# Gate 1 and the delta-rule mixer's gate as seven-product blocks, and what moves for it

## The reference, cut to what matters

```python
mod = jax.nn.silu(c) @ P['w_ada'] + P['b_ada']            # 12 groups of 512 columns
h = _rmsnorm(x, P['norm_mix_w']) * (1.0 + sc_m) + sh_m
proj = h @ P['w_in']     # u_a, qkv_b, z_b, a_b, b_b, x_c, gate_c, z_d, xbc_d, dt_d, gate_raw
# delta rule, chunks of 64 in the reference, 128 in the kernel; g, beta per token and head
kk = k k^T ; lhs = I + strict(beta * kk * decay) ; sol = lhs^-1 [v beta, k beta exp(g)]
u = sol_v - sol_k S ; o = (q exp(g)) S + (q k^T * decay) u ; S = S exp(g_end) + k_end^T u
o = o * rsqrt(mean(o*o) + EPS) * P['gdn_norm_w'] * silu(z)          # z_b is the mixer's gate
gates = sigmoid(gate_raw)             # four gates of 1024 channels: gate0 to gate3
out = sum(gates * branches) @ P['w_out']
```

## Time and profile before

| | |
|---|---|
| median of runs | 2577.1 us (2575.58 to 2579.7) |
| the profiled execution | 2580.41 us, span 2578.6 us |
| PE busy | 2415.3 us, 94% |
| DVE / ACT / POOL busy | 1124.6 / 787.4 / 545.0 us |
| PE, gate 1 (L660) | 151.5 us busy, 768 records of 192 columns |
| PE, units (L704) | 671.2 us busy, 2688 records of 288 columns |
| PE, tiles (L541) | 515.3 us busy, 1584 records of 384 columns |

### The profile page before, as it was taken

How to read it: one execution, slowest core, us unless ns; L and a number is a source line. 1 busy time by engine, 2 the same in 40 slices (tenths; PEclk the granted TensorE clock), 3 DMA queues, 4 the chain that set the end, 5 groups by cost and what they waited for, 6 DMA issues and landing times.

```text
span 2578.6 us, 41253 instructions
## 1 busy us (share of the span) xinstructions
PE 2415.3 (94%) x16732; PEld 1619.7 (63%) x16732; DVE 1124.6 (44%) x1802; ACT 787.4 (31%) x1507; POOL 545.0 (21%) x524
## 2 busy tenths in 40 slices
PE   5999899999999999999999999999987999989994
PEld 3555888885677777776777755555464444434443
DVE  4355555553362565984959912333452111101115
ACT  3132222221123222336477531110142222222224
POOL 0000000003466344665744500000000000000003
PEclk9999999999999999999999999999997999999997
DMA  7000123203111111411101252223036466767436
GB/s 326 33 33 33 46 81 111 79 29 111 70 33 49 47 63 65 166 33 51 72 31 56 80 223 106 106 106 114 1 139 270 152 238 245 296 236 268 154 131 232
DMA packets 71908, 304.20 MB, mean 118 GB/s; under 512 B 9693, under 2 KB 35877, under 8 KB 48421
## 3 DMA queue, kind: packets, MB, share of 16 engines
q1 hardware_dynamic: 59620, 267.98, 27.7%
q0 software_dynamic: 8928, 22.03, 2.5%
q10 hardware_dynamic: 3168, 11.54, 1.1%
HBM read 699.18 MB, written 63.71 MB: 296 GB/s over the span
## 4 chain that ended last, share of the span: by engine, by line
PE 79%; DMA 8%; DVE 5%; ACT 4%; issue 2%; SPq 1%; POOL 1%; ACTq 0%; DVEq 0%; POOLq 0%
PE psum L704 22%; PE psum L541 20%; PE psum L1666 8%; DMA arena<-in_moe 7%; PE psum L1524 4%; PE psum L1650 4%; PE psum L660 4%; PE psum L1241 2%; ACT arena L1990 1%; PE psum L570 1%; PE psum L1127 1%; PE psum L1103 1%; PE psum L1635 1%; PE psum L1229 1%; PE psum L1461 1%
## 5 line engine op out<-in xcount | busy, mean ns | idle before, releaser
L704 PE MATMUL psum<-arena 128*128 128x288 f32 x2688 | 671.2, 410 | 12.7 <-ACT arena L785 8.4
L704 PEld LDWEIGHTS psum<-arena 128*128 128x128 f32 x2688 | 508.0, 191 | 163.5 <-issue 12.2
L541 PE MATMUL psum<-arena 128*128 128x384 f32 x1584 | 515.3, 488 | 5.7 <-issue 2.9
L541 PEld LDWEIGHTS psum<-arena 128*128 128x128 f32 x1584 | 300.9, 190 | 219.4 <-issue 9.6
L1666 PE MATMUL psum<-arena 128*32 128x256 f32 x5632 | 326.3, 388 | 36.2 <-DMA arena<-in_moe 35.0
L1666 PEld LDWEIGHTS psum<-arena 128*32 128x32 f32 x5632 | 179.3, 112 | 169.5 <-DMA arena<-in_moe 38.1
L2180 POOL TENSOR_TENSOR arena<-arena,cst 128x288 f32<-128x288 f32 (+1 forms) x204 | 180.5, 888 | 51.9 <-ACT cst L779 22.5
L2108 ACT ACTIVATE arena<-psum 32x512 f32<-32x512 f32 x174 | 102.4, 589 | 230.7 <-PE psum L1650 229.2
L1650 PE MATMUL psum<-arena 128*32 128x512 f32 x1408 | 162.5, 600 | 7.8 <-DMA arena<-in_moe 7.2
L779 ACT ACTIVATE cst<-psum 128x288 f32<-128x288 f32 x192 | 78.9, 412 | 249.0 <-PE psum L704 243.4
L660 PE MATMUL psum<-arena 128*128 128x192 f32 x768 | 151.5, 332 | 0.0
(11 more groups left out here) (563 smaller groups left out, 2902.3 us busy)
## 6 DMA issues: line engine op xcount, KB each, us to landing
arena<-in_moe SPq DMA_DIRECT2D x532, 1024.0 KB
arena<-in_ada SPq DMA_DIRECT2D x12, 2048.0 KB, 8.8
arena<-gate_raw SPq DMA_DIRECT2D x8, 2304.0 KB, 8.0
gate_raw<-arena SPq DMA_DIRECT2D x96, 144.0 KB, 1.8
arena<-in_gate SPq DMA_DIRECT2D x12, 1024.0 KB, 5.2
y_rows<-arena ACTq DMA_DIRECT2D x22, 512.0 KB
arena<-in_br SPq DMA_DIRECT2D x8, 1024.0 KB, 9.6
y_save<-arena SPq DMA_DIRECT2D x3, 2304.0 KB, 6.9
```

The lines of the kernel that those rows point to most:

```text
L541: last = nc.tensor.matmul(pset(s)[:, n, :], w[:, kk, :], src[:, kk, n * N3:(n + 1) * N3], start=(kk == 0), stop=(kk == K - 1))
L704: last = nc.tensor.matmul(bank(6 + i % 2)[:, 0:NQ4], w[:, k, :], x[:, k, :], start=(k == 0), stop=(k == 3))
```

## The change: what it does

- Gate 1 and zb become units. The loop's fill is now the first token half (h = 0) of gates 1, 3 and 2: 12 units, 336 matmuls of 288 columns, one pair of tiles and half of the tokens at a time. The second halves come later, so these weights are loaded twice. Units in all: 48 before, 60 after.
- GpSimd works from the end of the first stage on: three forms of the first token half, after all modulation rows, then the one in place when the last qkv tile is filled, then sums for every unit of the loop, the unit's additions, and the squares' addition (k's place += v's place) of chunks 0 to 7. After the loop it makes the second half's forms, when the store of the prompt's state is done; VectorE copies the first half's forms to their later place.
- The modulation groups 4 to 11 are made in the first stage, one at each of the qkv tiles 2 to 9: its rows ahead of the tile, its columns ahead of the tile's last third (`pe_tile` now yields there).
- The short sequences' state is loaded over v's place in QKV.
- Behind the loop come zb, xbc and two units of gate 2; zd moves into the middle loop with the second halves of gates 1 and 3, its silu after chunks 2, 3, 5, 6. In the LRU stage one unit stands behind each of the four tiles. ScalarE's eviction of ua's first pair waits for two LRU tiles and not for four.
- ScalarE squares the outputs of the chunk before ahead of the exponentials, and its evictions lag by one product in the first solves (LAGGED).

```diff
-STREAM = [("xbc", 0), ("xbc", 1), ... ("gate0", 2), ("gate0", 3)]
-UNITS = [(a, p, h) for a, p in STREAM for h in range(2)]
+VISITS = [("gate%d" % k, p, (0,)) for k in (1, 3, 2) for p in range(4)]
+LOOP_UNITS = len(VISITS)
+VISITS += [("zb", 0, BOTH), ("zb", 1, BOTH)] + [("xbc", p, BOTH) for p in range(4)] + [("gate2", 0, (1,)), ("gate2", 1, (1,))]
+VISITS += [("zd", 0, BOTH), ("zd", 1, BOTH)] + [("gate%d" % k, p, (1,)) for k in (1, 3) for p in range(4)]
+VISITS += [("xc", 0, BOTH), ("xc", 1, BOTH), ("gc", 0, BOTH), ("gc", 1, BOTH), ("gate2", 2, (1,)), ("gate2", 3, (1,))]
+VISITS += [("ua", 0, BOTH), ("ua", 1, BOTH)] + [("gate0", p, BOTH) for p in range(4)]
...
-        counts = [("start", 13 if last else 17), ("ops", 4)]
+        counts = [("start", 4 if last else 12), ("ops", 2 if last else 3)]
...
-            counts += [("turn%d" % st, 2), ("right%d" % st, 1)]
-            counts += [("step%d_%d" % (st, i), 1) for i in range(st == SOLVE - 1 and not last, steps - (last and st == len(STEPS[c])))]
-        counts += [("w", 2), ("o", 2)] if last else [("w", 0), ("o", 0)]
-        counts += [("head%d" % h, 8) for h in range(GH)] if last else [("next", 2)]
+            counts += [("turn%d" % st, 1 if last else 2), ("right%d" % st, 1)]
+            counts += [("step%d_%d" % (st, i), 0 if last else 1)
+                       for i in range(st == SOLVE - 1 and not last, steps - (last and st == len(STEPS[c])))]
+        counts += [("w", 1 if last else 2), ("o", 1 if last else 0)]
+        counts += [("head%d" % h, 5) for h in range(GH)] if last else [("next", 4)]
...
+LAGGED = ("turn1", "right1", "turn2", "right2", "right3") + tuple("step%d_%d" % (st, i) for st in (1, 2, 3) for i in range(3))
...
 # TensorE, first stage
             for m in range(12):
+                t = m - 2
+                ada = 0 <= t < LATE
+                if ada:
+                    pe.wait_ge(s_awl, 16 * (t + 1))
+                    if t:
+                        pe.wait_ge(s_mod, t)
+                    if t == 5:
+                        pe.wait_ge(s_zero, 2)
+                    ada_rows(pe, 7 if t < 5 else 6, AWL)
...
-                    pe_tile(pe, "qkv", m, w[:, m % 4], HT, KD)
+                    for _ in pe_tile(pe, "qkv", m, w[:, m % 4], HT, KD):
+                        if ada:
+                            pe.wait_ge(s_aev, ADA_EARLY + t + 1)
+                            ada_cols(7 if t < 5 else 6, 0, adaL)
...
 # TensorE, in a unit
+                if u == LOOP_UNITS:
+                    pe.wait_ge(t_moved, 1)
+                if new:
                     pe.wait_ge(u_sums, FORMS[(2, h)])
-                if h == 0:
+                if FIRST[u]:
                     pe.wait_ge(u_sums, sums_no(n, 2))
...
 # ScalarE
+                if c:
+                    act_out_squares(c - 1)
                 act.wait_ge(c_diff, c + 1)
...
+                take(max(GDN_COUNT[(c, tag)] // 4 - (tag in LAGGED) - at, 0))
+                dst = QKV[:, 8:12, c * P:(c + 1) * P] if c != NC7 - 1 else hd(late_sq, 4)
...
+            take(7 * LOOP_UNITS + 7 - at)
+            act_root(S, "gdn_ss", 0, rt_n, 1.0 / P, rms_eps)
...
+                if c in (2, 3, 5, 6):
+                    act_silu_y("zd", (2, 3, 5, 6).index(c))
...
 # GpSimd
-            wait_phase(pool, 2)
+            pool.wait_ge(s_arow, ADA)
+            forms(0, loop_forms)
+            wait_fill(pool, "qkv", 11)
+            form_in_place(0)
+            for _ in sums(0):
+                pass
             for u in range(len(UNITS)):
+                if u < LOOP_UNITS:
+                    for c in range(NC7):
+                        if u == -(-(GDN_COUNT[(c, "next")] + 4) // YIELDS):
+                            add_squares(c)
+                if u == LOOP_UNITS:
+                    wait_phase(pool, 2)
+                    pool.wait_ge(p_st, 16)
+                    forms(1, tforms[1])
+                    form_in_place(1)
...
 # SP, in the loop
+            for u in range(LOOP_UNITS):
+                sp_store_gates(sp, u)
+                after_unit(u)
+                load_visit(sp, u + 3)
+                if u == 9:
+                    sp.wait_ge(q_add, NC7 - 1)
+                    sp.wait_ge(c_tok, NC7)
+                    sp.dma_start(QKV[:, 8:12, 0:NP_TOK], A["gdn_state"][0].rearrange("p (j c) -> p j c", j=4)).then_inc(s_w[1], 16)
             sp.wait_ge(c_ss, NC7)
-            sp.dma_start(A["gdn_p"], cS).then_inc(s_pstate, 16)
+            sp.dma_start(A["gdn_p"], cS).then_inc(p_st, 16)
...
 # VectorE, behind the loop
+            for a, b in zip(tforms[0], loop_forms):
+                last = nc.vector.tensor_copy(a, b)
+            V.then(last, t_moved)
```

478 lines of the change are left out of this document (221 added, 257 removed), and 8 rows, old and new, of tables (HALF_LOADS, STREAM).

## The result

The changed kernel takes 2590.68 us (median of 5 runs, 2590.18 to 2595.44) against 2577.1 before (5 runs): ratio 1.0057, interval 1.0043 to 1.0072. That is 13.6 us slower, where 8.5 us faster was forecast, and it lies outside the range. The profiled execution has a span of 2588.9 us, 10.3 more than the one of before.

The account below looks back on a forecast made before the run. TensorE, busy 94% of the span, was taken as the bound. Terms 22.5 + 20.8 + 0 + 7 - 36.5 + 0.5 - 22.8 = -8.5 us gave 2571.9 profiled, 2568.6 median; range 2555 to 2584.

Parts of the forecast that it names:

- the lock in the loop: Delta-rule loop: VectorE's operations with two SBUF inputs wait for GpSimd's additions; 0.5 us a chunk (bounds 0 and 5).
- rival A: Chunk's chain from c_cols to c_ops and c_ss: uncovered port-lock waits cost 2.5 us a chunk, 2587 us; chance 0.17.
- The fill itself: Delta-rule loop's chunks: longer filling products and moved modulation add 1.9 us a chunk (1.6 to 2.2), +2.7 bare.
- the evictions: Loop's chunks: ScalarE's evictions sit between copies that a chain waits for; 0.2 us a chunk (0 to 1).
- ops: Place in a loop chunk where TensorE waits 1.0 us for VectorE's L2380, so longer fill costs 0 there.
- The last chunk: Loop's last chunk: fewer fill yields, but its start already waits for VectorE; 0 (-3 to +4).
- The loop's start: Before chunk 0: GpSimd's form and sums delay VectorE's last convolution, 5.5 us, late fill 1.5; +7 (2 to 12).
- Behind the loop: Stretch from the loop to the middle loop: fewer units and cheaper squares, less new waits; -36.5 us.
- The form wait: Behind the loop: GpSimd's second-half forms await gdn_p's store, so TensorE waits 3.6 us (0 to 9).
- Middle loop: Middle loop: zd's four silus with table changes come in, mostly covered by VectorE's idle time; +0.5 us (0 to 4).
- LRU: LRU stage: two units fewer, -27.2, but 4.4 us more wait behind tile 2; -22.8 us (-25 to -19).
- First stage: First stage: eight modulation groups enter, each about 2.75 us, plus 0.5 for ScalarE's copy; +22.5 us.

Follow-up runs that it names:

- e1: Changed kernel with GpSimd's additions for the loop's units (weight sums but the first visit's, partial products) cut to 4 columns each; 2565.2 us, ratio 0.9960.
- k2: Changed kernel with no lagged evictions: ScalarE evicts products in the levels' places as soon as due; 2591.6 us, ratio 1.0055.
- j1: Changed kernel with GpSimd's first four weight sums and in-place form held back until VectorE has copied chunk 0's columns; 2591.9 us, ratio 1.0070.
- j4: Changed kernel with the weight sums of the visits behind the loop, from the second on, cut to 4 columns; 2582.9 us, ratio 1.0032.
- f2: Changed kernel with the store of the prompt's delta-rule state queued behind the load after unit 10, not behind unit 11; 2591.6 us, ratio 1.0064.

## Why the prediction was wrong

- **The step that failed is the size of the lock in the loop** ("At 0.4 us and a chance of a third to a half each: 0.5 us a chunk"). It measured 1.8 (e1), over 7 chunks 12.3 us for 3.5. The row it stood on the earlier trace rows showed the mechanism and its price with one addition of 128x288, but the loop's visits bring four of 128x512 at 1335 ns. And the cover was too small: "four of them (L2360 to L2367) have 1.0 us of cover". The product of 512 columns among these four grew by 0.46 us on average, and the two small ones L2382 and L2388 by 0.96 together, as much each as a wide one; with 1.4 us more than before, TensorE waits 4.2 us before L1180 in five of the seven chunks. Nor did I ask when in the chunk the additions run; rival A named that place and got 0.17. With its own 2.5 us a chunk it had the mechanism and was nearer in size, though too high; that its total (2587) came near 2590.7 is in part luck, for it holds nothing of the middle loop's 6.0.
- The Trainium skill's rule, SBUF — State Buffer, section "SBUF: two separate sides", is that of an exclusive lock for the whole instruction. What the runs show agrees with it: the two-piece and four-piece sums, with more GpSimd time, cost less (39.79 and 39.77 us a chunk for 40.88). I had weighed it and then used a mean.
- The fill itself: +2.6 us a chunk without the lock (e1), forecast 1.9 and 0.2 for the evictions. The 0.2 was about right: TensorE's waits for ScalarE are 1.4 us in seven chunks, and k2 gives back 0.3 a chunk. The 0.5 missing is cover that wasn't there: I had the bare work at +2.7 and let 0.8 of it fall into waits, but in e1 TensorE is busy 2.6 us a chunk more and idle for 5.3 us of the seven chunks, as before (5.2). The 1.00 us of the earlier trace rows that I took for TensorE's wait at "ops" is that of its weight load; its products waited 0.7.
- The last chunk: 0 forecast within -3 to +4, +2.8 measured, of it 2.9 the lock.
- The loop's start: chunk 0 grew by 7.0, forecast 9.6 (7 and its chunk's part). The cause, the last convolution locked, was the one named; holding the additions back gave 3.9 (j1) of the 5.5 that I took for it.
- Behind the loop: -33.2 for -36.5. The form wait was right, and the old waits, 5.4 us in all, did go, but 2.6 of others came. TensorE's busy time fell by 34.8 us, not 37.1: TensorE ran at 1.2 GHz for 10.2 us here and for 3.4 before, 6.8 of them from about the form wait's end. With the loop units' additions cut short the stretch took 213.8, 2.4 less (e1).
- Middle loop: +6.0 for +0.5, outside my 0 to 4. I counted zd's silus (0.5, measured 1.9) and not that the tail's gating products would meet more sums. The same step failed again.
- LRU: -19.7 for -22.8, inside its bounds. TensorE's busy time fell by the 27.2 forecast; TensorE's idle time grew by 7.5 us for 4.4. j4's 140.7 puts 4 us on the sums.
- First stage: +20.7 for +22.5, right in mechanism and near in size. Ranges: the sum of bounds I gave for the lock alone (0 to 5 us a chunk) reached 40 us, and the range's upper end of 2584 did not carry that.

Together: forecast -8.5, profiled +10.3. The misses: chunks 1 to 7 +12.5, chunk 0 -2.6, chunk 8 +2.8, first stage -1.8, behind +3.3, middle +5.5, LRU +3.1, rest -4.0: 18.8.

Open: why single edits (f2, j1) moved the profile's stage and not the median, while several together did (each has four runs, and its interval reaches about as far as the gain); when TensorE's clock falls; and which of GpSimd's additions delays each chunk, since chunks differ (39.3 to 42.9 us in the changed kernel), the longest by 1.2 GHz behind a wait.

## What to carry to other kernels

Before work is moved to GpSimd beside a chain of VectorE, list VectorE's SBUF-only operations on the chain, tiny ones too. Here each took 0.4 to 0.5 us more on average beside additions of 1.3 us, and at worst one can wait a whole addition. Add this up along the chain and set it against the cover that the chain has at that place. Then cut that length (two pieces), or hold the work back until VectorE reads PSUM. A saving of TensorE work counts only where TensorE stays the bound: here 20 us less work made 13.6 us more time, and 2573 came only after the additions were shorter or held back. And a wait of TensorE can cost more than its own length: from about the end of three of them here (1.9, 4.3 and 3.2 us) it ran at 1.2 GHz for 3.4 to 6.8 us.
